# Filler tiles that give each operand tile of the projections its own start address, in a two-model float32r kernel

## What is computed

```python
h = rms_norm(x, norm1_w[l]);  proj = h @ w_in[l]
...
up = h @ ffn_w_up[l]
gate, val = jnp.split(up, [D_FF], axis=-1)
x = x + (jax.nn.gelu(gate) * val) @ ffn_w_down[l]
...
def swiglu_ffn(h, w_gate, w_up, w_down):
    return (jax.nn.silu(h @ w_gate) * (h @ w_up)) @ w_down
# second model, each of DEPTH_2 = 2 layers
h = swiglu_ffn(rmsnorm(x, g[0]), ffn_w_gate[l, 0], ffn_w_up[l, 0], ffn_w_down[l, 0])
x = x + 0.5 * rmsnorm(h, g[1])
h = hybrid_mixer(rmsnorm(x, g[2]), w_in[l], ...)
x = x + rmsnorm(h, g[3])
h = swiglu_ffn(rmsnorm(x, g[4]), ffn_w_gate[l, 1], ffn_w_up[l, 1], ffn_w_down[l, 1])
x = x + 0.5 * rmsnorm(h, g[5])
```

## Time and profile before

| | us |
|---|---|
| median of 3 runs | 1479.03 |
| lowest, highest | 1478.87, 1481.07 |
| span of the profiled execution | 1479.1 |
| TensorE busy (its matmuls) | 1452.4 |
| VectorE, ScalarE busy | 966.4, 735.9 |

### The profile page before, as it was taken

The page is one execution under the profiler, slowest core; times in us unless marked ns, Lnnn a source line. Parts: engine busy times, 40 slices in busy tenths (PEclk is TensorE's granted clock), DMA queues, the critical chain, the costliest instruction groups (busy, mean ns, idle before and its releaser), DMA issues. The chain is left out here.

```text
span 1479.1 us, 21371 instructions
## 1 busy us (share of the span) xinstructions
PE 1452.4 (98%) x8920; PEld 1269.6 (86%) x8920; DVE 966.4 (65%) x1163; ACT 735.9 (50%) x936; POOL 90.7 (6%) x106
## 2 busy tenths in 40 slices
PE   7999999999999999999999999999999999999998
PEld 7899999899998788888987888878888898788886
DVE  6867786678864666555886666557565578765644
ACT  5533863555553544435665444445444466544442
POOL 0000000000000000000540000000000035000000
PEclk9999999999999999999999999999999999999999
DMA  7735455666655476554523755556654473366542
GB/s 250 239 115 171 143 192 184 173 179 189 181 188 183 146 243 222 185 185 137 151 98 119 237 177 196 170 172 224 220 196 152 141 190 105 118 210 190 180 162 95
DMA packets 251415, 259.14 MB, mean 175 GB/s; under 512 B 26662, under 2 KB 213431, under 8 KB 251319
## 3 DMA queue, kind: packets, MB, share of 16 engines
q1 hardware_dynamic: 250432, 255.49, 54.4%
q10 hardware_dynamic: 884, 2.28, 0.4%
HBM read 256.69 MB, written 1.05 MB: 174 GB/s over the span
## 5 line engine op out<-in xcount | busy, mean ns | idle before, releaser
L1000 DVE TENSOR_TENSOR w_lo<-raw,w_hi 128x2048 fp32r<-128x2048 f32 x240 | 546.0, 2277 | 327.3 <-ACT w_hi L606 327.0
L606 ACT ACTIVATE w_hi<-raw 128x2048 fp32r<-128x2048 f32 x240 | 456.3, 1901 | 343.5 <-PE psm L1678 161.8
L1678 PE MATMUL stream<-a_hi,w_hi 128*128 128x256 f32 x1072 | 307.5, 287 | 2.7 <-DVE a_lo L1019 1.4
L1678 PE MATMUL stream<-a_hi,w_lo 128*128 128x256 f32 x1072 | 304.6, 284 | 0.0
L1678 PE MATMUL stream<-a_lo,w_hi 128*128 128x256 f32 x1072 | 304.6, 284 | 0.0
L1678 PE MATMUL stream<-w_hi,a_hi 128*128 128x512 f32 (+1 forms) x576 | 225.7, 392 | 8.1 <-DVE w_lo L1000 5.7
L1678 PE MATMUL stream<-w_hi,a_lo 128*128 128x512 f32 (+1 forms) x576 | 221.5, 385 | 0.0
L1678 PE MATMUL stream<-w_lo,a_hi 128*128 128x512 f32 (+1 forms) x576 | 221.0, 384 | 0.0
L1678 PEld LDWEIGHTS stream<-a_hi,w_hi 128*128 128x128 f32 x1072 | 206.9, 193 | 5.1 <-issue 2.8
L1678 PEld LDWEIGHTS stream<-a_lo,w_hi 128*128 128x128 f32 x1072 | 207.0, 193 | 0.1
L1678 PEld LDWEIGHTS stream<-a_hi,w_lo 128*128 128x128 f32 x1072 | 207.0, 193 | 0.0
(11 more groups left out here) (291 smaller groups left out, 1725.9 us busy)
## 6 DMA issues: line engine op xcount, KB each, us to landing
raw<-in_ffn_w_up SPq DMA_DIRECT2D x136, 512.0 KB, 5.0
raw<-in_ffn_w_down SPq DMA_DIRECT2D x104, 512.0 KB, 4.3
raw<-in_ffn_w_gate SPq DMA_DIRECT2D x88, 512.0 KB, 4.0
raw<-in_w_in SPq DMA_DIRECT2D x80, 512.0 KB, 4.6
raw<-in_w_out SPq DMA_DIRECT2D x24, 512.0 KB, 4.4
raw<-in_w_ret_o SPq DMA_DIRECT2D x8, 512.0 KB, 4.0
raw<-in_w_lru_o SPq DMA_DIRECT2D x8, 512.0 KB, 4.2
diag<-in_conv_diag SPq DMA_DIRECT2D x8, 512.0 KB, 5.7
```

Source lines behind the costliest of these rows:

```text
L606: nc.scalar.activation(w_hi[s][:, :, 0:n], raw[s][:, :, 0:n], ACT.Copy).then_inc(w_hi_ready, 1)
L1000: V.tensor_tensor(w_lo[s][:, :, 0:n], raw[s][:, :, 0:n], w_hi[s][:, :, 0:n].bitcast(F32), ALU.subtract).then_inc(w_split, 1)
L1678: return nc.tensor.matmul(dst, lhs, rhs, start=start, stop=stop, skip_group_check=True)
```

## The change

Unused filler tiles are allocated between the operand tiles, and the tile `pad` grows from 8 to 128 elements. No instruction is added, removed or moved on any engine; only start addresses differ.

```diff
-        a_hi, a_lo = sb("a_hi", [P, KT, T], F32R), sb("a_lo", [P, KT, T], F32R)
+        gap0 = sb("gap0", [P, 96])
+        a_hi = sb("a_hi", [P, KT, T], F32R)
+        gap1 = sb("gap1", [P, 16])
+        a_lo = sb("a_lo", [P, KT, T], F32R)
...
-        w_hi = [sb(f"w_hi{s}", [P, KT, UC], F32R) for s in range(NS)]
-        w_lo = [sb(f"w_lo{s}", [P, KT, UC], F32R) for s in range(NS)]
+        w_hi, w_lo = [], []
+        for tiles, name, gaps in ((w_hi, "w_hi", (112, 32, 32)), (w_lo, "w_lo", (16, 16, 40))):
+            for s in range(NS):
+                sb(f"gap_{name}{s}", [P, gaps[s]])
+                tiles.append(sb(f"{name}{s}", [P, KT, UC], F32R))
...
-        pad = sb("pad", [P, 8])
+        pad = sb("pad", [P, 8 + 120])
...
-        h_hi, h_lo = sb("h_hi", [P, NF1, T], F32R, scope=ff), sb("h_lo", [P, NF1, T], F32R, scope=ff)
+        h_hi = sb("h_hi", [P, NF1, T], F32R, scope=ff)
+        gap_h = sb("gap_h", [P, 64], scope=ff)
+        h_lo = sb("h_lo", [P, NF1, T], F32R, scope=ff)
```

## The result

Measured side by side on one chip, the changed kernel takes **1482.94 us** (median of 8 runs, 1482.44 to 1484.12), the kernel before 1479.77 (8 runs, 1478.18 to 1481.21). The ratio is 1.0023, 95% interval 1.0013 to 1.0033: 3.2 us slower, where 15.7 us faster was forecast. The time lies in the forecast's wide range (1450 to 1490) and on the wrong side.

The account below looks back on a forecast made before the run. TensorE's matmul pace was taken as the bound, busy 1452.4 of 1479.1 us. -14.3 - 7.4 + 13.0 - 7.0 = -15.7 gave 1463.4 us; own range 1456 to 1474, 8-in-10 range 1450 to 1490.

Parts of the forecast that it names:

- (f): Other engines: alignment kept and splits of the next unit still done in time, so zero effect.
- (a): 256-wide matmuls in feature_major: a_lo half a turn past a_hi saves 4.4 ns on each of 3216, -14.3 us.
- The turn: Float32r matmuls: each begins only when a turn of 32 cycles reaches the phase of its first address (128 bytes).
- (b): 512-wide passes, moving w tiles: shifted w_lo gains 4.4 ns in slots 0 and 2, slot 1 unchanged, -7.4 us.
- (c): 512-wide matmuls with a and b: 1941 leave distance 0 between moving and stationary tile, 6.7 ns each, +13.0 us.
- (d): 512-wide matmuls with h: slot 1 reaches distance 0 (-3.0), slots 0 and 2 gain the half turn (-4.0), together -7.0 us.
- (e): 256-wide matmuls leaving distance 0: costed at nothing because their weight load covers the whole matmul; otherwise +16.8 us.
- the second (only the distance, no turn): Rival: (c) and (d) pay +13.0 and -3.0, (a) and (b) zero, 1489.1 us; chance 0.21, 0.07 with 256-wide payments.
- The fourth: Rival: different distances per slot cancel, within 3 us of 1479; chance 0.17 shared with the rival that addresses don't matter.

Follow-up runs that it names:

- h_zero: Kernel before with pad 104 instead of 8 elements, so h_hi and h_lo start at the phase of the w tiles: 1470.17 us against 1478.92, ratio 0.9937.
- half_turn: Kernel before with a_lo, all w_lo and h_lo 64 bytes past their high tiles, h_hi at w_hi's phase: 1476.79 us against 1478.92, ratio 0.9983.
- views_lo: Kernel before with a and b placed 64 bytes further for 512-wide passes, and low tiles (except narrow a_lo, b_lo) 128 bytes later: 1464.24 us, ratio 0.9905.
- after_mod: Changed kernel with tiles moved by 256 bytes, so every phase modulo 256 stays: one execution, 1482.66 us.
- map_c: Kernel before with weight tiles of slots 0, 1, 2 at 224, 256, 320 bytes past a, h at a's phase: one execution, 1474.57 us against 1479.71.
- map_b: Kernel before with weight tiles of slots 0, 1, 2 at 128, 160, 192 bytes past a, h at a's phase: one execution, 1487.41 us against 1478.92.
- the maps: Three variants of the kernel before, each weight slot at another distance from a, high and low tiles at one phase: 1477.98, 1487.41 and 1474.57 us.
- lo_mix: Kernel before with w_hi and h 64 bytes past a, w_lo at 0, 128, 192 in slots 0, 1, 2: one execution, 1474.21 us against 1479.71.

## Why the prediction was wrong

The bound was right: apart from before's stretch at the lower clock, TensorE's pace is all that moved, and it accounts for the time. So was the reading that addresses matter, and (f): VectorE and ScalarE stayed within 1%. The two rules that the prediction quotes from the Trainium skill, page "SBUF — State Buffer", section "SBUF: two separate sides", and page "TensorE: Matmul & The Clock Gate", section "Step-by-step: what each phase is for", would have left the time at 1479.1. Of the operands of the matmuls with weights h_zero moved only the stationary tiles of the down projections, and it gained 8.8 us, so here the pace of a float32r matmul does depend on where the stationary tiles stand, which the second rule doesn't lead one to expect. Whether TensorE waited for another engine, which is what the first rule denies, no run here shows. The spacing of N/2.4 + 2.5 ns, which the prediction compares with streams of matmuls, is what the Trainium skill, page "TensorE: Matmul & The Clock Gate", section "Back-to-back issue gap", states for an isolated matmul; no row here shows an isolated one.

The prediction took the agreement of the span (1479.1) with the median (1479.03) as a sign that nothing lies around the span. Each run takes some 2 us more than its span, so that agreement was chance; the forecast difference of 15.7 us doesn't hang on it.

The steps by their letters:

(a) **The step that failed.** -14.3 was forecast; the 256-wide work gave -3.8 in all, of which 0.52 ns x 3312 + 2.2 ns x 288 = 2.3 us is pace; nearly all of the rest is before's stretch at the lower clock. No slot had the 115.6 ns of two short and one long start: they had 117.8, 120.5 and 119.8. The turn was built from numbers that fit it (exactly 32 cycles over, nothing over at 1.2 GHz, 1120 cycles for two matmuls of h), but none of the float32r rows had two successive moving tiles at unlike phases; half_turn had them in every slot and gave 117.8 and 231.1. What the runs show in the turn's place is a pace that follows the relations of the tiles modulo 256 bytes: with a_lo 64 bytes past a_hi and the distances at 0 the gain is 2.1 ns, half of the forecast 4.4 (slot 0, half_turn), and at the other distances of slots 1 and 2 it is gone.

(b) It was to bring -7.4 and has the wrong sign. 512-wide matmuls got slower wherever high and low tiles stood at unlike phases: +3.4 ns in half_turn (231.1 for 227.7), +3.5 in views_lo. Whether that comes from the successors or from the tiles of one product is not shown.

(c) The sign was right, and that a distance costs; that its 13.0 us lie near the measured +10.4 of (b) and (c) together (+4.5 ns on the mean of 2496) is in part luck. It was 6.7 ns for each of 1941 matmuls. The table by distance shows 228 at 0, 229.5 at 64 and 232 to 234 elsewhere, so 4 to 6 ns there, and the prediction wrote distances modulo 512, where after_mod and map_c show 256. Modulo 256 only 4 of the 9 pairs leave 0 and not 7: slot 0 keeps all three (and has 231.6, near the 231.1 of half_turn, whose relations modulo 256 it has), slot 1 loses all (232.6, as 232.2 at distance 128 in map_b), slot 2 has one pair off and successors 32 apart (232.9). Each slot loses nearly the same though the three stand differently.

(d) h was to gain 7.0 and gained 3.6 us. Slot 1, now alike in all tiles modulo 256, does reach the expected 226.6, but only after ten matmuls at 232; in a unit of 24 that leaves 229.3 on average. Such settling was in the earlier trace rows and was put down to the four transposes; it also comes when the relation of the phases changes from slot to slot, here at each of the slot's units and in map_c's slot 1 (five matmuls there). Giving each slot a phase of its own pays it at every unit. Slots 0 and 2 gained 1.8 and 2.6 ns instead of 4.4.

(e) Against before, slots 1 and 2 of the 256-wide work changed by +0.6 and -0.1 ns, so nothing seems lost. But slot 0, where the distances stayed 0, gained 2.1, and half_turn shows that all slots would have. So what these two slots' distances took away, 2.7 and 2.0 ns, belongs in (e). That no single distance costs the 256-wide work anything in the maps shows that the two effects do not simply add. The reason given, a weight load that already covers the whole matmul, was not shown. The mean load of the whole family got shorter, 193 to 189 ns, but that does not tell what sets what:

```profile
L1686 PEld LDWEIGHTS stream<-a_lo,w_hi 128*128 128x128 f32 x1072 | 202.5, 189 | 0.1
```

This answers to the earlier trace rows.

Of the rivals, the second (only the distance, no turn) had the right sign, and the mechanism for part of the loss: slot 0 kept its distances modulo 256 and lost as much. It was 6 us too high at 1489.1: its price per matmul was 6.7 for the map's 4 to 6, and it gave the 256-wide work nothing. The fourth, a mix that cancels slot by slot, named the right kind of cancelling, slot against slot and family against family, and missed its bound of 3 us narrowly (3.2 side by side).

Redone with what the runs measured: 2496 x 4.5 = +11.2 for the wide passes with a and b, 1344 x -2.7 = -3.6 and 3600 x -0.65 = -2.3, together +5.3. The trace has +3.0; of the 2.3 between them, 1.6 are before's stretch at the lower clock and the rest lies in distances that hold waits.

What stays open is why a distance of 64 bytes is worth 16 cycles to a 256-wide matmul, why the pace of a matmul depends on those before it, and which relation counts when high and low tiles differ: that of the tile loaded beside the moving one, that of the one multiplied with it, or that of successors. The traces show starts alone, and no run tells where inside the chip the time goes. More kernels with a_lo and w_lo at unlike phases would be needed.

Plain float32 did not respond. The convolution's products came to stand at other phases in these kernels (`diag` less `up`, modulo 256: 32 bytes before, 96 after, 224 in half_turn), and twelve of them take 2.86 us in all three. First after, then half_turn:

```profile
750.82 2.86 PE L1686 MATMUL ps<-up,diag 128*128 128x256 f32 x12
```

```profile
745.56 2.86 PE L1686 MATMUL ps<-up,diag 128*128 128x256 f32 x12
```

## What to carry to other kernels

When TensorE bounds a float32r kernel, measure starts of matmuls against their columns: 32 or more cycles over may be a matter of tile addresses, and a filler tile of some hundred bytes tells (h_zero: -8.8 us). Keep all operand tiles of one family of matmuls at one relation, the same in every buffer slot, since a relation that changes from unit to unit pays a settling of five to ten matmuls each time. Test each matmul width for itself, and run the kernel several times before believing a pace: the same program can run in two rhythms. Before two traces are compared to the microsecond, compare their granted clock in windows and not only by slices: here a stretch of 3 us at half the clock was a third of the change's effect.

## What was not expected of the hardware

- The pace of float32r matmuls depends on operand addresses with a period of 256 bytes: 226.4 to 234 ns for 512 columns, 113.3 to 121 for 256.
- More than one relation counts: with high and low tiles at one phase, the distance of weight and activation tile (h_zero, the maps); with unlike ones, 512 columns take 231.1 ns even when every tile loaded beside a moving one stands at distance 0 (half_turn, views_lo), and in lo_mix up to 3.8 ns more than the distances by themselves would give.
- The two widths want different distances: 256 columns 64 bytes (113.3 ns, 272 cycles), 512 columns 0 (226.7 ns, 544 cycles).
- A rhythm carries over from matmul to matmul: ten matmuls of some 232 ns before 226.4 after a change of slot, and at 64 bytes two lasting rhythms of 113.3 and 117.8 ns, between which one program chose differently in two executions. 512 columns have two as well where high and low tiles differ (231.3 and 233.0 ns in lo_mix).
- Plain float32 products took the same 2.86 us for twelve at three different relations of their tiles.
